# Retention, sparse attention and experts on one core: the norms' inverse roots multiplied behind the products, other work inside the norms, ten expert slots

## The chip, the cores and the metric

The kernel runs on one core of a Trainium2 chip. The metric is the device time of one execution in microseconds (us); the kernel before takes 2245.85 us, the median of three runs. A core has TensorE (PE; its weight loads are shown apart, as PEld), VectorE (DVE), ScalarE (ACT), GpSimd (POOL) and SyncE (SP), which run side by side and wait for one another on semaphores. SP and ACT also issue the transfers; all of these share 16 DMA engines.

## What is computed

Two blocks over 256 tokens of width 1024, everything in float32. The first has a retention mixer, a gated feed-forward layer (FFN), a sparse-attention mixer with shared keys and values, and a second FFN. The second has a gated mixer (a spatial branch and a windowed attention that also reads 256 context tokens), and 16 experts that each take 32 tokens. Every layer is wrapped in norms:

```python
h = x
for layer in range(2):
    if layer == 1:
        shared = nsa_shared_kv(h, kv_norm, ...)        # rms_norm(h, kv_norm) @ kv_w
    normed = rms_norm(h, mix_norm_pre[layer])
    mixed = retention_mixer(normed, ...) if layer < 1 else nsa_mixer(normed, ..., shared)
    h = h + rms_norm(mixed, mix_norm_post[layer])
    normed = rms_norm(h, ffn_norm_pre[layer])
    gate, up = split(normed @ w_in)
    h = h + rms_norm((silu(gate) * up) @ w_out, ffn_norm_post[layer])
...
h1 = modulate(rmsnorm(x, norm1_g), sh1, sc1); hc = modulate(rmsnorm(ctx, norm1_g), csh1, csc1)
x = x + g1 * ((g_a * (y_a @ w_proj_a) + g_b * (y_b @ w_proj_b)) @ w_out)
h2 = modulate(rmsnorm(x, norm2_g), sh2, sc2)
x = x + g2 * expert_choice_ffn(h2, w_router, w_gate, w_up, w_down)   # 16 x 24 MB of weights
```

`rms_norm(x, g)` is x * rsqrt(mean(x*x)) * g over the 1024 features of a token.

## The kernel before, in words

Features lie on the 128 partitions in 8 chunks of 256 tokens, so a sum over features is a product with a matrix of ones: `norm(n)` is 8 float32 products of `sq` with `ones` into bank 4 of PSUM. ACT takes the root (`roots`), DVE the reciprocal (`inverse`, into `rs`).

Dense weights come in units of 1 MB (`load`) through a ring of six slots (`RING`), issued by SP in order. Each unit is split into two rounded halves for the fast matmul: ACT copies (`split_hi`), DVE subtracts (`split_lo`), with two buffers each; a ring slot is free when its low half is made, a split buffer when PE has finished the unit (`used`). Tokens are split the same way into `x_hi` and `x_lo`. A unit is then 48 matmuls: `col_products` (with `col_T`, `col_tok`) for columns of a weight, line 616 of the profile; `wide_tok` (24 matmuls of 512 columns, line 640); `row_T` for rows of a weight, line 653, which accumulates 8 output chunks in four PSUM banks.

A seam between two layers runs as `post` and `pre`: squares of the four PSUM banks, `norm`, root, reciprocal, `xn` = product * gain * `rs` (DVE), `h += xn` (POOL, `residual`, line 2039), squares of `h`, `norm`, root, reciprocal, `xn` = h * gain * `rs`, the split of `xn`, and only then the first product of the next layer. This happens at N_POST0/N_PREF0, N_POSTF0/N_PRE1, N_POST1/N_PREF1 (where the context's norm N_CTX stands between the two) and N_POSTF1/N_IN2.

An FFN has 11 steps of three units: gate and up columns, and the rows of the output weight of the step before. ACT takes silu from PSUM, DVE multiplies by up (`hidden`), and both split the result into `f_hi`, `f_lo`, one pair for all steps. The eight steps in the middle are a hardware loop.

In the second block the mixer's products are ordered v, u (`ua`), q, keys (unit 12, for own tokens and context), then the spatial products, then values (unit 13). Keys are copied across partitions by 8 small DMAs (`kd2`, line 1460) before the windowed attention; its gates are computed inside the attention. Then `w_proj_a` (PA), `w_proj_b` (PB), the gated sum (POOL adds, line 2059) and `w_out` (WO), the router, the choice of tokens (`xe`) and the experts.

The experts' weights are 192 loads of 2 MB (`load_expert`) through `ERING` = 8 slots: seven can be issued before the tokens are chosen, the eighth (`late_expert_slots`, whose last part lies over the split operands) after the last product that reads those. From then on load g waits until PE has used load g - 8 (`e_used`).

Small tables (a bias table of 3 MB written to DRAM with each row repeated 128 times, `bias_skew`; norm gains; router weights) are moved by ACT's queue.

## Time and profile before

| | us |
|---|---|
| three runs | 2242.27, 2245.85, 2246.39 |
| the profiled execution, its own time | 2246.82 |
| its span | 2245.0 |
| PE busy / DVE / ACT / POOL | 1707.0 / 675.8 / 577.4 / 135.2 |
| 0 to 1310 us | the dense layers, 1 MB weight units |
| 1310 to 2227 us | the experts |

An execution's time is the span and 1.8 us around it. The profile has a page (busy time of each engine, the span in 40 slices, the DMA queues, the chain of work that ended last), and the trace behind it can be asked for a stretch, an engine or a line. TensorE's granted clock is given as a share of 2.4 GHz: 1.00 is that level, 0.50 is 1.2 GHz. "<-" names what ended an idle time.

### The profile page before, as it was taken

How to read it: one execution, taken by the hardware profiler on the slowest of the kernel's cores; microseconds unless marked ns; L12 is line 12 of the kernel's file. 1: busy time of each engine (PE TensorE's matmuls, PEld its weight loads, DVE VectorE, ACT ScalarE, POOL GpSimd, SP SyncE). 2: the span in 40 equal slices, each digit the busy share in tenths (PEclk: the TensorE clock that was granted, in tenths of full speed). 3: DMA queues.
4: the chain of work that ended last, by engine and by line, in shares of the span. 5: the costliest groups of instructions: out<-in, count | busy, mean ns of one | idle time of the engine just before them, and what ended most of it. 6: DMA issues, size and time to landing. Idle time of an engine off the chain costs nothing.

```text
span 2245.0 us, 27132 instructions
## 1 busy us (share of the span) xinstructions
PE 1707.0 (76%) x11760; PEld 1186.1 (53%) x11760; DVE 675.8 (30%) x973; ACT 577.4 (26%) x962; POOL 135.2 (6%) x153
## 2 busy tenths in 40 slices
PE   7998899979888999697888665566565555656655
PEld 7898799968557999595678631111111111111111
DVE  4644454454546444462555310000000000000001
ACT  3354344433654343341554210000000000000000
POOL 1101100010221000100321000000000000000000
PEclk8999899979999999898999788887878787888778
DMA  9843455528582555353126269999999999999995
GB/s 233 271 148 113 159 170 186 187 76 245 215 309 93 182 176 187 112 169 94 57 76 241 116 278 428 427 428 428 428 428 428 427 427 428 429 426 428 429 427 246
DMA packets 160620, 603.54 MB, mean 269 GB/s; under 512 B 9542, under 2 KB 114151, under 8 KB 132711
## 3 DMA queue, kind: packets, MB, share of 16 engines
q1 hardware_dynamic: 147712, 587.23, 66.9%
q10 hardware_dynamic: 12808, 14.85, 3.1%
q8 instruction: 79, 1.29, 0.2%
q14 instruction: 21, 0.17, 0.0%
HBM read 594.71 MB, written 4.19 MB: 267 GB/s over the span
## 4 chain that ended last, share of the span: by engine, by line
PE 51%; DMA 38%; DVE 5%; ACT 3%; POOL 1%; issue 1%; ACTq 0%; DVEq 0%
PE ps L616 20%; DMA late_expert_slots<-in_w_exp_down 13%; DMA late_expert_slots<-in_w_exp_gate 13%; PE ps L653 12%; DMA late_expert_slots<-in_w_exp_up 11%; PE ps L640 3%; PE ps L1133 3%; PE ps L600 2%; DVE split_operands L538 2%; PE ps L995 1%; PE ps L1154 1%; POOL residual L2039 1%; DVE inv_root L1567 1%; PE ps L804 1%; PE ps L983 1%
## 5 line engine op out<-in xcount | busy, mean ns | idle before, releaser
L616 PE MATMUL ps<-split_operands 128*128 128x256 f32 x3744 | 466.1, 287 | 18.8 <-DVE split_operands L561 14.4
L616 PEld LDWEIGHTS ps<-split_operands 128*128 128x128 f32 x3744 | 460.8, 194 | 21.8 <-issue 21.0
L538 DVE TENSOR_TENSOR split_operands<-dense_ring,split_operands 128x1024 fp32r<-128x1024 f32 x288 | 353.4, 1269 | 352.0 <-ACT split_operands L530 352.0
L530 ACT ACTIVATE split_operands<-dense_ring 128x1024 fp32r<-128x1024 f32 x288 | 288.1, 1050 | 286.0 <-PE ps L653 161.1
L2007 DVE TENSOR_TENSOR arena<-arena,ps 128x512 f32<-128x512 f32 x16 | 11.0, 688 | 870.8 <-PE ps L1133 870.8
L1133 PE MATMUL ps<-late_expert_slots,arena 128*32 128x512 f32 x768 | 131.0, 817 | 103.9 <-DMA late_expert_slots<-in_w_exp_gate 53.6
L1133 PE MATMUL ps<-dense_ring,arena 128*32 128x512 f32 x768 | 125.6, 789 | 80.3 <-DMA dense_ring<-in_w_exp_gate 41.9
L653 PE MATMUL ps<-split_operands 128*128 128x256 f32 x1152 | 148.5, 294 | 26.4 <-DVE split_operands L548 17.6
L653 PEld LDWEIGHTS ps<-split_operands 128*128 128x128 f32 x1152 | 147.3, 203 | 28.5 <-issue 15.5
L653 PE MATMUL ps<-hidden_split,split_operands 128*128 128x256 f32 x1056 | 134.4, 289 | 8.4 <-DVE split_operands L538 8.4
L653 PEld LDWEIGHTS ps<-hidden_split,split_operands 128*128 128x128 f32 x1056 | 132.2, 196 | 8.8 <-issue 8.8
L1133 PEld LDWEIGHTS ps<-late_expert_slots,arena 128*32 128x32 f32 x768 | 24.6, 129 | 205.0 <-DMA late_expert_slots<-in_w_exp_gate 84.7
L1133 PEld LDWEIGHTS ps<-dense_ring,arena 128*32 128x32 f32 x768 | 25.5, 130 | 180.3 <-issue 77.2
L1154 PE MATMUL ps<-dense_ring,arena 128*32 128x512 f32 x384 | 68.2, 846 | 47.2 <-DMA dense_ring<-in_w_exp_down 44.8
L1154 PE MATMUL ps<-late_expert_slots,arena 128*32 128x512 f32 x384 | 63.2, 791 | 52.6 <-DMA late_expert_slots<-in_w_exp_down 52.6
L1553 ACT ACTIVATE arena<-ps 128x512 f32<-128x512 f32 x16 | 9.6, 597 | 301.3 <-PE ps L1154 301.3
L600 PE MATMUL ps<-squares,ones 128*128 128x256 f32 x192 | 59.0, 471 | 35.0 <-ACT squares L1180 35.0
L1547 ACT ACTIVATE arena<-ps 128x512 f32<-128x512 f32 x16 | 9.6, 597 | 291.3 <-PE ps L1133 291.3
L1551 ACT ACTIVATE arena<-ps 128x256 f32<-128x256 f32 x16 | 6.1, 383 | 298.4 <-PE ps L1139 298.4
L640 PE MATMUL ps<-split_operands 128*128 128x512 f32 x288 | 67.2, 395 | 6.9 <-DVE split_operands L561 6.9
L600 PEld LDWEIGHTS ps<-squares,ones 128*128 128x128 f32 x192 | 44.0, 237 | 47.9 <-ACT squares L1180 33.0
L1133 PE MATMUL ps<-dense_tables,arena 128*32 128x512 f32 x256 | 41.5, 779 | 35.4 <-DMA dense_tables<-in_w_exp_up 20.7
(272 smaller groups left out, 1599.9 us busy)
## 6 DMA issues: line engine op xcount, KB each, us to landing
dense_ring<-in_w_exp_gate SPq DMA_DIRECT2D x24, 2048.0 KB, 36.7
dense_ring<-in_w_exp_up SPq DMA_DIRECT2D x24, 2048.0 KB, 36.1
late_expert_slots<-in_w_exp_up SPq DMA_DIRECT2D x24, 2048.0 KB, 36.7
dense_ring<-in_w_exp_down SPq DMA_DIRECT2D x24, 2048.0 KB, 36.0
late_expert_slots<-in_w_exp_gate SPq DMA_DIRECT2D x24, 2048.0 KB, 35.9
late_expert_slots<-in_w_exp_down SPq DMA_DIRECT2D x24, 2048.0 KB, 36.4
dense_ring<-in_ffn_w_in SPq DMA_DIRECT2D x44, 1024.0 KB, 5.1
dense_ring<-in_ret_w_in SPq DMA_DIRECT2D x24, 1024.0 KB, 11.9
```

The lines of the kernel that those rows point to most:

```text
L530: act.activation(w_hi[:, n % 2, c], ring[U % RING][:, c], ACT.Copy).then_inc(hi_ready, 1)
L538: dve.tensor_tensor(w_lo[:, n % 2, c], ring[U % RING][:, c], w_hi[:, n % 2, c], ALU.subtract).then_inc(lo_ready, 1)
L600: mm = pe.matmul(ps[:, 4, 0:T], ones[:], sq[:, c, :], start=c == 0, stop=c == 7)
L616: mm = pe.matmul(ps[:, bank, b * T:b * T + T], left, right, start=k == 0 and i == 0, stop=k == 7 and i == 2)
L640: mm = pe.matmul(ps[:, banks[t], :], x[:, 4 * half + k, t * P:t * P + P], w[:, k, :], start=half == 0 and k == 0 and i == 0, stop=half == ...
L653: mm = pe.matmul(ps[:, bank0 + b // 2, (b % 2) * T:(b % 2) * T + T], w[:, c, b * P:b * P + P], v[:, c, :], start=first and c == 0 and i == ...
L804: mm = pe.matmul(ps[0:60, kind, 0:T], blocks[:, kind, 8 * w + c, :], slot8(U)[:, c, :], start=w == 0 and c == 0, stop=w == 1 and c == 7)
L983: mm = pe.matmul(ps[:, 5 + 2 * s, t * T:t * T + T], src[:, k, t * P:t * P + P], slot8(U_IN2 + 13)[:, k, :], start=k == 0, stop=k == 7)
L995: mm = pe.matmul(ps[:, 7, b * T:b * T + T], w[:, k, b * P:b * P + P], x[:, k, :], start=k == 0 and i == 0, stop=k == 7 and i == 2)
L1133: mm = pe.matmul(ps[32 * j:32 * j + 32, bank, :], xcur[:, k, :], sl[:, c, 512 * j:512 * j + 512], start=k == 0, stop=k == 7)
L1154: mm = pe.matmul(ps[32 * g:32 * g + 32, 6, :], e_hidT[:, m * P + 32 * (w - 8):m * P + 32 * (w - 8) + 32], sl[:, m, 512 * half:512 * half + ...
L1567: dve.reciprocal(rs[:], root[:]).then_inc(rs_ready, 1)
```

## The change

- **Inverse roots behind the products.** x_hi and x_lo are made from h * gain (`tokens_hi`, `gained_lo`), without the inverse root. The next layer's first two units start on them, interleaved by chunk (`pair_products`), and `norm(n)` stands between the first and second half of the second unit. The inverse root is multiplied where the products leave PSUM: into the rotation tables, the retention's gates (`g_scale`) and values (by token, `rs_tok`, after `turn_rs`), in the FFNs once on the gate ahead of silu (`gate`) and once on its result (`silu_scale`), and on keys and values (`kv_out`). This holds for N_PRE0, N_PREF0, N_PRE1 and N_PREF1; N_IN2 and N_MOE stay as they were.
- **Shorter norms.** Squares of a PSUM bank and the last updates of h start bank by bank (`acc_done`) during the last unit. DVE adds to h (`post`), no longer POOL. The retention's output product starts while the last head's norm runs, in banks 5, 6, 7, 4. The last hidden step of an FFN is split into `x_hi`/`x_lo` and so doesn't wait for `f_hi`.
- **Other work inside norms.** The two halves of the bias tables' products (`bias_table`), the context's sum of squares and the context's keys and values (`keys(ctxn)`, `values(ctxn)`) run on PE inside the seams. The context's norm itself runs on POOL during the second FFN. The bias table's write to DRAM and six small loads are issued during the first FFN (`small_loads`).
- **Order of the second mixer**: v, keys, values, u with the spatial products inside, q. The keys' DMAs are issued two units before q. The last rotation of q runs after the first scores. DVE makes the gated sum by bank.
- **Ten expert slots**: `ERING` = 10, three in the arena. Loads 2 to 8 go out at the points in the diff.

```diff
-ERING = 8
+ERING = 10
...
+ACC = {N_POST0: (5, 6, 7, 4), N_POSTF0: (4, 5, 6, 7), N_POST1: (0, 1, 2, 3), N_POSTF1: (0, 1, 2, 3)}
+TOLD = {N_POST0: 0, N_POSTF0: 3, N_POST1: 6, N_POSTF1: 9, U_PB: 12, U_WO: 15}
+SUM_BANK = {N_PRE0: 4, N_POST0: 0, N_PREF0: 4, N_POSTF0: 0, N_PRE1: 4, N_POST1: 4, N_PREF1: 0, N_POSTF1: 4,
+            N_IN2: 4, N_MOE: 4, N_END: 4}
...
+        e_slots = [arena_slots[0], ring_tail[:], arena_slots[1], ring_mem[:, 0, :], arena_slots[2]] + \
+            [ring_mem[:, i, :] for i in (1, 2)] + [late_slots[:, i, :] for i in range(3)]
...
+                    sp.wait_ge(xhi_ready, X_PA + 4)
+                    sp.wait_ge(xlo_ready, X_PA + 4)
+                    load_expert(2)
+            sp.wait_ge(lo_ready, 2 * SPLIT_NO[U_PB + 3] + 2)
+            load_expert(3)
+            sp.wait_ge(merged, 4)
+            load_expert(4)
+            for g, U in ((5, U_WO + 1), (6, U_WO + 3)):
                 sp.wait_ge(lo_ready, 2 * SPLIT_NO[U] + 2)
                 load_expert(g)
             sp.wait_ge(used, U_END)
-            for g in range(5, ERING - 1):
+            for g in range(7, ERING - 1):
                 load_expert(g)
             sp.wait_ge(xe_mm, 8)
             load_expert(ERING - 1)
...
+            def pair_products(U, banks, place, x0, between):
+                def chunk(v, k):
+                    hi, lo = parts_of(U + v)
+                    if k % 4 == 0:
+                        pe.wait_ge(lo_ready, 2 * SPLIT_NO[U + v] + k // 4 + 1)
+                    for b in range(2):
+                        for i, (w, x) in enumerate(((hi, x_hi), (hi, x_lo), (lo, x_hi))):
+                            left, right = place(b, w[:, k, :], x[:, k, :])
+                            mm = pe.matmul(ps[:, banks[v], b * T:b * T + T], left, right,
+                                           start=k == 0 and i == 0 and b == 0, stop=k == 7 and i == 2,
+                                           skip_group_check=True)
+                    return mm
+                for k in range(4):
+                    pe.wait_ge(xlo_ready, x0 + k + 1)
+                    chunk(0, k)
+                    chunk(1, k)
+                for k in range(4, 8):
+                    pe.wait_ge(xlo_ready, x0 + k + 1)
+                    mm = chunk(0, k)
+                mm.then_inc(used, 1)
+                between()
+                for k in range(4, 8):
+                    mm = chunk(1, k)
+                mm.then_inc(used, 1)
...
+                    if last and b in (1, 3, 5):
+                        mm.then_inc(acc_done, 1)
...
+            for u in range(8):
+                row_pair(U_RO, u, 8, X_RO, ACC[N_POST0], ((g_sc, 7), None, (g_sc, 8), (oroot, 4)))
+            norm(N_POST0)
             pe.wait_ge(on_ev, 4)
...
+                pair_products(U0, (gate_bank(f, 0), gate_bank(f, 0) + 1), by_feature, x0, lambda: norm(n))
...
+            pair_products(U_KV, (1, 3), by_feature, X_KV, lambda: norm(N_PRE1))
...
+            pe.wait_ge(ctx_squared, 1)
+            for c in range(8):
+                mm = pe.matmul(ps[:, 6, 0:T], ones[:], ctx_sq[:, c, :], start=c == 0, stop=c == 7)
+            mm.then_inc(ctx_sum, 1)
...
+            pe.wait_ge(ctx_ready, 2)
+            take(U_K)
+            keys(ctxn, 7).then_inc(kc_mm, 1)
             norm(N_IN2)
+            take(U_V)
+            values(ctxn, 6).then_inc(vc_mm, 1)
...
+            def tokens_hi(posted, name):
+                for k in range(DC):
+                    if posted is not None:
+                        act.wait_ge(h_ready, POST[posted] + k + 1)
+                    act.activation(x_hi[:, k, :], h[:, k, :], ACT.Copy, scale=col(name, k)).then_inc(xhi_ready, 1)
+                    if k % 2:
+                        act.activation(sq[:, k - 1:k + 1, :], h[:, k - 1:k + 1, :], ACT.Square).then_inc(sq_ready, 1)
...
+            def small_loads():
+                act.wait_ge(brow_ev, 1)
+                act.dma_start(bias_dram, bias_rows.unsqueeze(1).to_broadcast([HEADS, P, 384])).then_inc(bias_out, 16)
+                for dst, src in rests:
+                    act.dma_start(dst, src).then_inc(rest_in, 16)
...
+            def gained_lo(x0, name, k):
+                dve.wait_ge(xhi_ready, x0 + k + 1)
+                dve.scalar_tensor_tensor(out=x_lo[:, k, :], in0=h[:, k, :], scalar=col(name, k), in1=x_hi[:, k, :],
+                                         op0=ALU.mult, op1=ALU.subtract).then_inc(xlo_ready, 1)
...
+            def post(n, name, U, x0=None, next_name=None):
+                split_lo(dve, U)
+                split_lo(dve, U + 1)
+                inverse(n)
+                for k in range(11 if next_name else 9):
+                    if k < 8:
+                        dve.scalar_tensor_tensor(out=xn[:, k, :], in0=acc_chunk(ACC[n], k), scalar=col(name, k),
+                                                 in1=rs[:], op0=ALU.mult, op1=ALU.mult).then_inc(scaled, 1)
+                    if 1 <= k < 9:
+                        dve.wait_ge(scaled, POST[n] + k)
+                        dve.tensor_tensor(h[:, k - 1, :], h[:, k - 1, :], xn[:, k - 1, :],
+                                          ALU.add).then_inc(h_ready, 1)
+                    if next_name and k >= 3:
+                        gained_lo(x0, next_name, k - 3)
...
+                def gate(j, r=0):
+                    taken(dve, gate_unit(f, j), r)
+                    dve.tensor_tensor(halves(f_silu[:, j % 2, :]), halves(ps[:, gate_bank(f, j), :]), two(rs[:]),
+                                      ALU.mult).then_inc(f_gate, 1)
+                def silu_scale(j, r=0):
+                    dve.wait_ge(f_act, r * 2 + (base + j + 1))
+                    dve.tensor_tensor(halves(f_silu[:, j % 2, :]), halves(f_silu[:, j % 2, :]), two(rs[:]),
+                                      ALU.mult).then_inc(f_sc, 1)
...
+            dve.wait_ge(gt_sig, 2)
+            product_b(0)
+            product_b(1)
+            merge(0)
+            product_b(2)
+            merge(1)
+            pair_lo(dve, X_WO, 0, two_chunks(gb, 0))
+            product_b(3)
...
+                if k % 2 == 0:
+                    bank_of(U_WO, k // 2)
...
```

## Rows read from the trace of the kernel before

**Rows 1.** Table by stretch: busy us (instructions) of PE, PEld, DVE, ACT, POOL; clock, DMA share, GB/s.

```profile
300.00:400.00 100.00, 100.00 (x835) 100.00 (x834) 47.72 (x46) 40.17 (x46) 0.00 (x0) 1.00 0.55 179
...
1290.00:1300.00 10.00, 3.26 (x11) 2.80 (x12) 8.49 (x22) 0.00 (x0) 0.00 (x0) 0.50 0.00 0
...
1400.00:1500.00 100.00, 58.18 (x368) 14.91 (x372) 2.76 (x4) 2.95 (x6) 1.49 (x4) 0.82 1.01 428
```

**Rows 2.** Experts: the chain's last load (start, us, what); SP's issues of three loads.

```profile
2186.93 36.27 DMA late_expert_slots<-in_w_exp_down
...
1262.10 47.23 SPq L446 DMA_DIRECT2D late_expert_slots<-in_w_exp_up  x3
```

**Rows 3.** Timeline, start: start us, us, engine, line, what, [idle before].

```profile
18.95 2.00 ACT L530 ACTIVATE split_operands<-dense_ring 128x1024 fp32r<-128x1024 f32 x2 [9.96 <-DMA dense_ring<-in_ret_w_in]
20.97 1.28 ACT L1186 ACT_TABLE_LOAD   x1
22.27 0.38 ACT L1186 ACTIVATE root<-ps 128x256 f32<-128x256 f32 x1
...
31.72 47.69 PE L616 MATMUL ps<-split_operands 128*128 128x256 f32 x384 [4.32 <-issue]
```

**Rows 4.** Timeline, seam between the retention's heads and its output product.

```profile
189.71 1.89 PE L745 MATMUL ps<-squares,ones 128*128 128x256 f32 x8
200.40 48.48 PE L653 MATMUL ps<-split_operands 128*128 128x256 f32 x384 [8.80 <-DVE split_operands L538]
```

**Rows 5.** Timeline, seam to the first FFN.

```profile
249.57 3.72 PE L600 MATMUL ps<-squares,ones 128*128 128x256 f32 x16 [0.69 <-ACT squares L1180]
255.53 3.23 DVE L1655 SCALAR_TENSOR_TENSOR normed<-ps,cols,inv_root 128x256 f32<-128x256 f32 x8
270.68 26.29 PE L616 MATMUL ps<-split_operands 128*128 128x256 f32 x192 [4.00 <-DVE split_operands L561]
```

**Rows 6.** Timeline, last output unit of the first and of the second FFN.

```profile
462.45 8.50 PE L653 MATMUL ps<-hidden_split,split_operands 128*128 128x256 f32 x48 [4.21 <-DVE split_operands L538]
...
904.21 7.47 PE L653 MATMUL ps<-hidden_split,split_operands 128*128 128x256 f32 x48 [4.21 <-DVE split_operands L538]
```

**Rows 7.** DMA queues from 33 to 63 us: packets, MB, share of 16 engines.

```profile
q10 hardware_dynamic: 1873, 2.88, 85.2%
q1 hardware_dynamic: 998, 1.02, 9.6%
```

**Rows 8.** Timeline, shared keys and values: shift DMAs, the blocks made from them, the next products.

```profile
509.49 4.33 ACTq L1342 DMA_DIRECT2D arena<-arena  x6
522.83 3.75 DVE L1710 TENSOR_TENSOR arena<-arena,cols 128x480 f32<-128x480 f32 x4
530.39 14.02 PE L804 MATMUL ps<-dense_ring,arena 128*60 128x256 f32 x64
```

**Rows 9.** Timeline, seam to the second FFN.

```profile
713.59 25.13 PE L616 MATMUL ps<-split_operands 128*128 128x256 f32 x192 [6.45 <-DVE split_operands L561]
```

**Rows 10.** Timeline, second mixer: v, context keys, first scores, their maximum, first transposes.

```profile
936.18 23.47 PE L640 MATMUL ps<-split_operands 128*128 128x512 f32 x96 [6.88 <-DVE split_operands L561]
1015.01 7.07 PE L959 MATMUL ps<-arena,dense_ring 128*128 128x256 f32 x32
1057.04 2.08 PE L1005 MATMUL ps<-arena 64*128 64x512 f32 x4 [14.73 <-DMA arena<-arena]
1060.92 1.23 DVE L1889 TENSOR_TENSOR arena<-ps,tabs 128x1024 f32<-128x1024 f32 x1 [26.22 <-PE ps L1007]
```

**Rows 11.** Timeline, from PB over the merge and WO to the router's norm.

```profile
1222.03 2.48 DVE L1933 TENSOR_TENSOR arena<-arena,ps 128x512 f32<-128x512 f32 x4 [2.31 <-PE ps L653]
1230.30 8.58 PE L653 MATMUL ps<-split_operands 128*128 128x256 f32 x48 [8.38 <-DVE split_operands L548]
1243.08 18.98 PE L653 MATMUL ps<-split_operands 128*128 128x256 f32 x144 [4.20 <-DVE split_operands L548]
1267.94 1.75 DVE L1567 RECIPROCAL inv_root<-root 128x256 f32<-128x256 f32 x1 [2.61 <-ACT root L1186]
```

## What I predicted

> **What bounds the kernel now.** I read the busy table by stretch first. From 300 to 400 us PE is busy all the time at a granted clock of 1.00 (2.4 GHz) while DMA is at 0.55: the dense layers are bound by PE. From 1400 to 1500 us PE is at 58% and DMA at 1.01 with 428 GB/s: the experts are bound by their weights [rows 1]. The chain of waits says the same, and that the last load lands at 2223.2 [rows 2]. So a gain before 1310 us moves the whole expert stream forward, and a gain inside it comes only from loads made earlier. Then I read PE's timeline for idle time in the dense part: it stands at the seams [rows 3 to 11]. A unit at full clock is 5.76 us (48.49 for 8 units, less a slow start; 5.74 to 5.77 in the chain). R below is the end of PE's last product before a seam; hand-overs between engines cost 0.02 to 0.1 us and are in the steps.
>
> **Start.** Before, products start at 31.7, after the norm and the bias tables, and eight units take 47.69, which is 1.7 over 46.0 (half clock at first), so unit 2 starts at 44.9 [rows 3]. After: the weights land at about 18 to 19 as before, two units are split by 22 to 24, PE starts at 22.6, does 72 matmuls (8.6, and 2 of low clock) and the norm of 3.7 [rows 5] to 36.2 to 37, then the second half (2.9). The inverse (root 0.4, reciprocal 1.75), the tables' multiplication (0.9), a split (2.4) and a rotation (1.5) follow the norm, so unit 2 starts at 43.5, with a low clock after 4.4 idle (1.7) and a transposition of 0.3: about 45.5. Loss 0.6; bounds +3 and -3.
>
> **Retention heads.** `g_scale` (0.7) goes ahead of each silu. The path from a gate unit's end to the next head's output product is then 8.6 to 8.8 us (scale, silu, split, table load 1.28, root, reciprocal 1.75, multiplication 1.23) where PE has 8.9 of other work. Loss 0.5, bounds 0 and 2.
>
> **Output product of the retention.** The last head's norm leaves 8.80 idle and 48.48 for 46.05 of work [rows 4]. After, the first two pairs are split before that norm, and bank 4 comes last, so the norm (root 6 us after the last gate unit) is behind 4.3 us of products and two units. 11.5 less; 10 if bank 4 is waited for.
>
> **First FFN's seam.** Before, R is 248.88 and four units are done at 296.97, R + 48.1 [rows 5]. After: squares of three banks lie inside the last unit, norm to R + 3.75, root and reciprocal to R + 6.0. DVE then runs product (0.40, 8 in 3.23 [rows 5]), addition (0.37) and low half (0.40) for each chunk, so the first low half is there at R + 9.1 and the next every 1.17, less than the 1.44 PE needs for two chunks. The first half of the bias tables (15 small products and one; an estimate of 3 us, bounded by 6.5 at half clock) fills R + 3.8 to 7. The pair with the norm inside takes 11.5 + 3.75 and 1 for low clock: R + 25.3, four units R + 36.8. Gate scale, silu, second scale, up and split of step 0 end at R + 32, ahead of the first output unit at R + 36.8. 11.3 less; bounds 8 (half clock for all of the first chunks) and 13.
>
> **FFN steps.** Each gets two DVE operations of 0.7 more, 9.8 of DVE per 17.3. The low half of an output unit is ready 3.4 after the gate unit, 2.3 before PE wants it. Nothing.
>
> **FFN ends.** The last output unit waits 4.21 and takes 8.50 or 7.47 for 5.76 [rows 6]. The last hidden step no longer waits for the unit before, and is split 1.8 before it is wanted. 6.95 and 5.9 less.
>
> **The bias write inside the first FFN.** From 33 to 63 us this write's queue (q10) takes 85% of the DMA engines and the weights' queue gets 1.02 MB, one unit in 30 us [rows 7]. It survived because six units had landed. After, it is issued at about R + 45, when six units ahead of PE have landed; unit 12 lands at about R + 80 and is wanted, split, at R + 82.9. Six small loads follow in the same queue. I take 1, bounds 0 and 8. The Trainium skill, "DMA: Bandwidth & Descriptors", Queues, rings and completion order, says that each DMA engine goes round the queues packet by packet; by that the weights would have got as many packets as the write, and this would cost nothing. The rows don't agree: 998 packets against 1873 with four loads waiting.
>
> **Shared keys and values.** Before, their next products start at 530.4, R + 59.4 with R = 470.95 [rows 6, 8]. After, the pair is done at R + 25.5, then unit, transposition, unit, a wait of 1.3 for `kv_out` behind `pre`, two units: R + 50.2. The shift DMAs are issued from P + 8 to P + 13.5 (P is the pair's end, 0.7 each); blocks are made 9 after the last issue as before, and take 3.75 [rows 8]: P + 26.4, R + 51.9. 7.6 less; bounds 4 (the bias read of 2 MB ahead of them in the queue) and 9.5.
>
> **Second FFN's seam.** R = 689.94, four units before at 738.72, R + 48.8 [rows 9]. After, as in the first, with the context's sum (3.7) as filler: R + 36.5. 12.3 less; bounds 9 and 13.5. The context's squares on ACT fall while PE is on the first output unit.
>
> **Second mixer.** R = 911.68. The maximum of the first scores starts at 1060.9, R + 149.2, after 14.73 idle for the keys' DMAs [rows 10]. After: keys of the context to R + 10.7, norm to 14.4 (the last squares are at 13.1), values to 21.3; modulated tokens arrive at R + 21.4. From there PE has v 21.9, keys and values 13.8 (7 each [rows 10]), eight units 46.1, spatial 3.6, four turns 3.5, scores 2.1, half a gate unit 2.9, a turn 0.9: 94.8. Each split on the way is ready in time, the nearest by 1.5, and the keys' DMAs by 14. But the last rotation (2.2) stands ahead of the maximum on DVE: R + 118.5. 30.7 less: 14.7 the DMAs, 13.8 context products now inside the norm, 3.1 an earlier start, 1.7 clock, less 2.6 for the rotation in front. Bounds 24 and 33.
>
> **Merge and output.** PB ends at 1222.0, WO at 1262.06, with 8.38 and 4.20 idle and 27.6 for 23.0 of work [rows 11]. After, three banks are multiplied and two added inside PB's last unit; the first split pair is ready at +1.7, unit 2 at +7: end at +24.7. 15.4 less; bounds 12 and 17. The router's norm starts on banks: inverse at W + 4.25 (W is WO's end) instead of 5.9. 1.6 less. The router's own chain (to 1310) stays.
>
> **Ten slots.** The eighth load is issued at 1309.3 [rows 2]; from 1290 to 1300 DMA moves nothing [rows 1]. Up to the last landing, 185 loads take 913.9 us, 4.94 each. After it is 183: 9.9 less. If the two more aren't landed in time it is 0; against that speak 35 idle us, hence 8 to 9.9.
>
> **Sum.** -0.6 - 0.5 + 11.5 + 11.3 - 1 + 6.95 + 5.9 + 7.6 + 12.3 + 30.7 + 15.4 + 1.6 + 9.9 = 111. The steps take every hand-over at its best, so I take 3 off: 108 from the profiled execution's 2246.8 is 2138.8. The median of the runs stands 1.0 below it: 2138.
>
> The Trainium skill, "ScalarE: Activation LUTs", What ACT_TABLE_LOAD costs, adds a drain of about 1.38 us to each 1.28 of a table switch. At the start the root follows its load by 0.02 [rows 3], so I count none. By the page three seams, where the root's load now ends only 0.25 after the norm, would each be 1.4 later, and the time 2142.
>
> **Rivals.**
> (a) The weights starve: if fewer than six units have landed when the bias write starts, each one missing is worth up to 5.8 of PE, and the small loads add some. 2144 to 2152. For: the margin of 3. Against: the same depth sufficed at the start. Chance 0.12.
> (b) The new DVE order sets the pace: splits queue behind waiting scales, rotations and merges, and low clock returns at each seam. Taking the low bounds of the seams (8, 4, 9, 24, 12) the sum is 25 lower: 2150 to 2165. For: eleven waits are new in DVE's queue. Against: DVE is at 48% [rows 1]. Chance 0.2.
> (c) The extra slots bring nothing because the stream's start is set by the last slot: 2147. Chance 0.05.
> (d) Slower than before: in the FFN steps gate, silu, second scale and up become a chain that PE waits for. There are 22 steps; from 4.9 us per step it eats the 108. PE waited for none of it in 300 to 400 us, and 2.3 or more are free at each step. 2250 to 2290, chance 0.02.
> (e) More than I count, with fewer low-clock stretches: 2115 to 2126. Chance 0.06.
> Forecast, 2126 to 2148: 0.55.
>
> **Numbers.** The range 2122 to 2158 leaves out (d), half of (b) and part of (e). A run of this kernel can tell about 0.2% from no change; all but (d) and some mishap are far below that: faster 0.97, same 0.01, slower 0.02.
>
> **What would show it.** Idle ahead of the first output unit of the retention under 1; four FFN units done at R + 37; no idle ahead of an FFN's last unit; no wait on DMA in PE's rows for the first FFN (else (a)); scores' maximum at R + 118; WO's end 25 after PB's; nine loads issued ahead of the choice of tokens, 4.94 each after. I'm wrong if PE waits on DVE rows for scales, or if the expert stream's first release isn't about 100 us earlier.

## The result and the profile after

The changed kernel takes 2167.6 us (median of four runs, 2165.1 to 2172.3) against 2246.0 before: ratio 0.966, interval 0.9636 to 0.9678. It is faster by 78 us where I had forecast 108, and it lies 10 us above my range of 2122 to 2158. Its profiled execution took 2165.05 with a span of 2163.3; the numbers below are of that one.

I first laid the two timelines side by side by the steps of the prediction. R is again the end of TensorE's (PE's) last product ahead of a seam.

| stage | predicted gain | measured gain |
|---|---|---|
| start, to the end of the query and key units | -0.6 | +2.3 |
| retention heads | -0.5 | 0.0 |
| retention's output product | 11.5 | 10.3 |
| first FFN's seam | 11.3 | 10.6 |
| first FFN behind it, its end included | 6.95 - 1 | **-21.7** |
| shared keys and values | 7.6 | 8.8 |
| second FFN's seam | 12.3 | 11.4 |
| second FFN behind it | 5.9 | 3.6 |
| second mixer, to the merge | 30.7 | 29.9 |
| merge and output | 15.4 | 15.4 |
| norm and choice of the router | 1.6 | 3.4 |
| experts | 9.9 | 9.8 |
| tail | 0 | -2.1 |
| sum | 111 - 3 | 81.7 |

Twelve of the thirteen lines are within 3 us of the forecast. One is off by 28, and that is the whole miss; the other twelve come to 103.4 for 105.1. (The sum is the difference of the two spans, 2245.0 - 2163.3.) The seams look as they were worked out. These are PE's rows of the changed kernel, at the retention's output product and the first FFN's seam (start us, us, engine, line, what, [idle before]); they answer to [rows 4, 5]:

```profile
201.44 34.81 PE L731 MATMUL ps<-split_operands 128*128 128x256 f32 x288 [0.65 <-DVE split_operands L581]
236.09 3.61 PE L639 MATMUL ps<-normed_and_squares,ones 128*128 128x256 f32 x16
...
245.06 10.85 PE L684 MATMUL ps<-split_operands 128*128 128x256 f32 x72 [0.16 <-DVE split_operands L1718]
255.74 3.61 PE L639 MATMUL ps<-normed_and_squares,ones 128*128 128x256 f32 x16
259.01 3.22 PE L684 MATMUL ps<-split_operands 128*128 128x256 f32 x24
262.07 11.68 PE L662 MATMUL ps<-split_operands 128*128 128x256 f32 x96
```

The idle 8.80 is 0.65 now. Behind R = 236.3 the four units are done at 273.75, R + 37.5, where I had R + 36.8; the norm's sum (3.61) stands inside the products. The second mixer and the output product, which answer to [rows 10, 11]:

```profile
889.67 7.07 PE L1024 MATMUL ps<-arena,dense_ring 128*128 128x256 f32 x32
896.57 3.62 PE L639 MATMUL ps<-normed_and_squares,ones 128*128 128x256 f32 x16
900.03 7.07 PE L1031 MATMUL ps<-dense_ring,arena 128*128 128x256 f32 x32
...
995.83 1.13 PE L1096 MATMUL ps<-arena 64*128 64x512 f32 x4
...
1168.16 23.30 PE L731 MATMUL ps<-split_operands 128*128 128x256 f32 x192 [1.45 <-DVE split_operands L581]
```

The context's products (7.07 each) lie around the norm's sum, the scores at 995.83 no longer wait for the keys' DMAs (14.73 before), and the output product has 1.45 of idle time for 8.38 and 4.20.

Then the first FFN. The stretch 300 to 400 us, in which PE was busy for all of 100.00 at a clock of 1.00 [rows 1], now reads (busy us and instructions of PE, PEld, DVE, ACT, POOL; clock, DMA share, GB/s):

```profile
300.00:400.00 100.00, 81.96 (x671) 81.96 (x672) 47.55 (x49) 35.20 (x40) 0.00 (x0) 0.89 0.61 175
```

PE's timeline has the hole, and it names a VectorE (DVE) split as what ended it:

```profile
318.04 7.38 PE L731 MATMUL ps<-hidden_split,split_operands 128*128 128x256 f32 x48 [27.01 <-DVE split_operands L571]
```

The last releaser need not be the cause, so I went back one engine more. ScalarE (ACT) in the same stretch; ACTq is its sequencer issuing DMAs:

```profile
279.75 0.68 ACTq L1437 DMA_DIRECT2D bias_skew<-arena  x1
280.46 8.10 ACTq L1439 DMA_DIRECT2D dense_tables<-in_nsa_w_in  x1
...
288.60 22.75 ACTq L1439 DMA_DIRECT2D dense_tables<-in_cmp_w_k  x2
...
313.26 0.98 ACTq L1439 DMA_DIRECT2D sink<-in_attn_sink  x1
314.54 2.00 ACT L563 ACTIVATE split_operands<-dense_ring 128x1024 fp32r<-128x1024 f32 x2 [32.40 <-issue]
```

The bias write itself is issued in 0.68 us. The six small loads behind it take ScalarE 33.8 us to issue, and from 282.1 to 314.5 it does no work and makes no high halves for PE. The chain of waits in this stretch (start, us, what) goes through the issues and not through any weight:

```profile
288.60 12.60 ACTq L1439
301.23 10.12 ACTq L1439
...
314.54 1.06 ACT split_operands L563
```

In the kernel before, the same six were issued from 253.7 on, where no bias write was under way, in 0.41 to 0.60 us each; the first:

```profile
253.72 0.41 ACTq L1280 DMA_DIRECT2D dense_tables<-in_nsa_w_in  x1
```

The hole costs 27.0 of idle time and 1.6 of low clock behind it (7.38 for a unit of 5.76): 28.6. The 6.95 at this FFN's end did come, hence -21.7. Without the hole the median would be 2139.

### The profile page after: what moved, and what is told of

Its sections match the earlier page's. It is cut to its first block, busy times and chain, and to the rows that moved or that the text cites. A ratio compares the mean times of both kernels' runs of the same rounds, so it can differ in the third digit from the quotient of the medians.

```text
span 2163.3 us, 27150 instructions
## 1 busy us (share of the span) xinstructions
PE 1676.8 (78%) x11764; PEld 1163.9 (54%) x11764; DVE 708.9 (33%) x1020; ACT 579.4 (27%) x959; POOL 111.1 (5%) x123
## 4 chain that ended last, share of the span: by engine, by line
PE 49%; DMA 39%; DVE 5%; ACT 3%; ACTq 1%; issue 1%; POOL 1%; SPq 0%; DVEq 0%
PE ps L662 18%; DMA dense_tables<-in_w_exp_gate 13%; DMA dense_tables<-in_w_exp_up 13%; DMA dense_tables<-in_w_exp_down 13%; PE ps L731 12%; PE ps L716 3%; PE ps L684 2%; PE ps L1224 2%; DVE split_operands L571 2%; PE ps L639 1%; PE ps L1085 1%; ACTq L1439 1%; PE ps L1245 1%; ACT split_operands L563 1%; DMA dense_ring<-in_ret_w_in 1%
## 5 line engine op out<-in xcount | busy, mean ns | idle before, releaser
L662 PE MATMUL ps<-split_operands 128*128 128x256 f32 x3360 | 413.9, 284 | 6.6 <-DVE arena L1776 4.1
L662 PEld LDWEIGHTS ps<-split_operands 128*128 128x128 f32 x3360 | 407.9, 193 | 8.1 <-issue 4.6
L1224 PE MATMUL ps<-dense_ring,arena 128*32 128x512 f32 x624 | 101.2, 781 | 77.0 <-DMA dense_ring<-in_w_exp_gate 39.5
L1224 PE MATMUL ps<-late_expert_slots,arena 128*32 128x512 f32 x592 | 104.7, 843 | 71.4 <-DMA late_expert_slots<-in_w_exp_gate 36.4
L731 PE MATMUL ps<-split_operands 128*128 128x256 f32 x1248 | 154.1, 286 | 7.2 <-DVE split_operands L581 7.2
L731 PEld LDWEIGHTS ps<-split_operands 128*128 128x128 f32 x1248 | 152.7, 195 | 9.0 <-issue 6.4
L1224 PE MATMUL ps<-arena 128*32 128x512 f32 x624 | 96.4, 745 | 62.0 <-DMA arena<-in_w_exp_gate 35.2
L731 PE MATMUL ps<-hidden_split,split_operands 128*128 128x256 f32 x960 | 120.0, 285 | 27.8 <-DVE split_operands L571 27.8
L731 PEld LDWEIGHTS ps<-hidden_split,split_operands 128*128 128x128 f32 x960 | 118.0, 194 | 28.2 <-DVE split_operands L571 28.2
L1224 PEld LDWEIGHTS ps<-dense_ring,arena 128*32 128x32 f32 x624 | 20.0, 127 | 153.4 <-DMA dense_ring<-in_w_exp_up 54.5
L1224 PEld LDWEIGHTS ps<-late_expert_slots,arena 128*32 128x32 f32 x592 | 19.5, 133 | 150.6 <-DMA late_expert_slots<-in_w_exp_up 52.6
L1224 PEld LDWEIGHTS ps<-arena 128*32 128x32 f32 x624 | 20.5, 123 | 132.9 <-issue 69.0
L1245 PE MATMUL ps<-arena 128*32 128x512 f32 x304 | 51.1, 805 | 34.3 <-DMA arena<-in_w_exp_down 28.8
L1245 PE MATMUL ps<-late_expert_slots,arena 128*32 128x512 f32 x320 | 51.6, 777 | 33.6 <-DMA late_expert_slots<-in_w_exp_down 31.2
L684 PE MATMUL ps<-split_operands 128*128 128x256 f32 x384 | 55.9, 312 | 23.3 <-DVE split_operands L571 18.6
L1245 PE MATMUL ps<-dense_ring,arena 128*32 128x512 f32 x288 | 47.0, 784 | 29.9 <-DMA dense_ring<-in_w_exp_down 28.3
```

The costliest lines, as they stand in the source:

```text
L662: mm = pe.matmul(ps[:, bank, b * T:b * T + T], left, right, start=k == 0 and i == 0, stop=k == 7 and i == 2)
L684: mm = pe.matmul(ps[:, banks[v], b * T:b * T + T], left, right, start=k == 0 and i == 0 and b == 0, stop=k == 7 and i == 2, skip_group_che ...
L731: mm = pe.matmul(acc_chunk(banks, b), w[:, c, b * P:b * P + P], v[:, c, :], start=first and c == 0 and i == 0 and b % 2 == 0, stop=last an ...
L1224: mm = pe.matmul(ps[32 * j:32 * j + 32, bank, :], xcur[:, k, :], sl[:, c, 512 * j:512 * j + 512], start=k == 0, stop=k == 7)
L1245: mm = pe.matmul(ps[32 * g:32 * g + 32, 6, :], e_hidT[:, m * P + 32 * (w - 8):m * P + 32 * (w - 8) + 32], sl[:, m, 512 * half:512 * half + ...
```

## Experiments

All ratios are to the kernel before, run on the same chip in turn; the interval is 95%. Two kernels that did not run in the same turn are compared by their medians, and their ratios can put the difference up to 2.8 us elsewhere; where a trace settles a size, it is given. "The small loads first" is the base of most of the later runs.

### What holds the issue

**The small loads first.**

```diff
 def small_loads():
+    for dst, src in rests:
+        act.dma_start(dst, src).then_inc(rest_in, 16)
     act.wait_ge(brow_ev, 1)
     act.dma_start(bias_dram, ...).then_inc(bias_out, 16)
-    for dst, src in rests:
-        act.dma_start(dst, src).then_inc(rest_in, 16)
```

> The changed kernel with one edit: ScalarE issues the six small loads (gate, compression and router weights, sink) ahead of the bias write and not behind it. In the changed kernel TensorE is idle for 27.0 us at 318.04, behind a VectorE step that waits for ScalarE, and ScalarE's own queue shows the bias write issued at 279.75 and the six small loads behind it until 313.3, two of them at 22.75 us together where before they took 0.4 to 0.6 us each. Theory A, ScalarE is held while it issues a load behind the bias write's many small packets: with nothing behind the bias write the 28.65 us are back, 2167.6 - 28.7 = 2139 us (ratio to before 0.952 to 0.953), no idle time over 3 us between 280 and 320, the six issues 0.4 to 1 us each. Theory B, the FFN's weights starve in the DMA queues under the bias write (my rival a of the prediction): the order of ScalarE's issues is no matter, an idle time of 20 to 30 us stays there, on the weights' wait, and the time stays at 2160 to 2168.

Measured: 2137.4 us, ratio 0.9533 (0.9517 to 0.9549). ScalarE's issues in this kernel:

```profile
280.69 0.40 ACTq L1437 DMA_DIRECT2D dense_tables<-in_nsa_w_in  x1
...
283.32 0.89 ACTq L1437 DMA_DIRECT2D sink<-in_attn_sink  x1
284.25 0.68 ACTq L1439 DMA_DIRECT2D bias_skew<-arena  x1
```

None of ScalarE's issues takes 1 us, PE has no idle time in this FFN, and the part behind the seam takes 167.04 us for 195.67. Theory A holds and B falls: the same bytes are issued within 5 us of the same time, and only the order of seven instructions differs.

**Two loads behind it**, the sink (8 KB) and one compression weight (64 KB), the other four ahead.

> As the run with the small loads first, but the two smallest in bytes of them (the sink and the second compression weight of the values) stay behind the bias write. What holds the issue is then told apart. Theory A1, the hold lasts until the bias write's own packets have room again, whatever comes behind: the first of the two is held some 8 to 30 us, and the time is 2150 to 2168. Theory A2, the hold goes by what the loads themselves bring (in the changed kernel the sink behind five others took 0.98 us, the four weight loads 8 to 12 each): the two are issued in under 5 us together and the time is 2139 to 2144. Theory B: 2160 to 2168 with the idle time on the weights' wait.

Measured: 2149.6, ratio 0.9590 (0.9569 to 0.9612).

```profile
282.58 0.94 ACTq L1439 DMA_DIRECT2D bias_skew<-arena  x1
283.56 12.38 ACTq L1441 DMA_DIRECT2D sink<-in_attn_sink  x1
295.97 3.95 ACTq L1441 DMA_DIRECT2D cmp_w_v<-in_cmp_w_v  x1
```

A1 holds by the hold; the time is 0.4 us under its range. The sink took 0.98 as the last of six and takes 12.38 as the first, longer than the 192 KB load in the same place of the changed kernel (8.10): the size of the load that is held matters less than how lately the bias write was issued. Some 16 us of hold leave 11.96 of idle time on PE.

**The kernel before, with its six small loads right behind its own bias write at the start** (they were issued 223 us later).

```diff
     act.dma_start(bias_dram, ...).then_inc(bias_out, 16)
+    for dst, src in rests:
+        act.dma_start(dst, src).then_inc(rest_in, 16)
     ...
-    for dst, src in rests:
-        act.dma_start(dst, src).then_inc(rest_in, 16)
```

> The kernel before with one edit: its six small loads, issued there at 253.7 to 257.0 in 0.4 to 0.6 us each, are issued right behind the bias write at the start (30.3), as the changed kernel does it later. Theory A: ScalarE is held there for 25 to 33 us, a stretch in which it has the start's evictions and activations to do, TensorE idles for most of it, and the time is 2246 + 15 to 30 = 2261 to 2276 us (ratio 1.007 to 1.013); small loads of 0.4 to 0.6 us each would refute it. Theory B: no hold of the issues, the weights of the start are late by at most some us, time 2243 to 2250.

Measured: 2277.6, ratio 1.0158 (1.0141 to 1.0174), 36 us slower than before. That is more than I had put down, and A's mechanism:

```profile
30.75 11.63 ACTq L1220 DMA_DIRECT2D dense_tables<-in_nsa_w_in  x1
42.42 20.11 ACTq L1220 DMA_DIRECT2D dense_tables<-in_cmp_w_k  x2
...
67.89 42.72 PE L616 MATMUL ps<-split_operands 128*128 128x256 f32 x336 [28.79 <-DVE split_operands L538]
```

The hold (34.7 us) is not a matter of this change's other parts: it came at both places where the six stood behind this write.

**The bias write issued by GpSimd (POOL)**, at nearly the same point (275.8 for 279.8); ScalarE's six loads stay where the change has them.

```diff
-    act.dma_start(bias_dram, ...).then_inc(bias_out, 16)
+pool.wait_ge(f_hidden, 2)
+pool.dma_start(bias_dram, ...).then_inc(bias_out, 16)
```

> The changed kernel with one edit: the bias write is issued by GpSimd at the same point of the first FFN, and ScalarE issues its six small loads where it did, now not behind it in its own queue. Theory A3, only the queue that took the bias write is full: ScalarE's issues take 0.4 to 0.9 us each, no idle time of TensorE at 280 to 320, time 2137 to 2140 (ratio 0.952 to 0.954). Theory A4, the hold comes from the 16 DMA engines themselves, which are busy with the bias write's small packets whoever issues them: ScalarE is held again for 10 to 30 us and the time is 2150 to 2168.

Measured: 2165.9, ratio 0.9641 (0.9622 to 0.9660), with 24.45 of idle time on PE. A3 falls; the time is in A4's range, and the hold of 31.8 us just over A4's 30. ScalarE's issues, with nothing large in its own queue:

```profile
280.29 0.40 ACTq L1437 DMA_DIRECT2D dense_tables<-in_nsa_w_in  x1
280.73 4.06 ACTq L1437 DMA_DIRECT2D dense_tables<-in_cmp_w_k  x1
284.82 3.89 ACTq L1437 DMA_DIRECT2D dense_tables<-in_cmp_w_k  x1
288.73 18.77 ACTq L1437 DMA_DIRECT2D cmp_w_v<-in_cmp_w_v  x1
```

From 282 to 312 us the queues of this kernel were (packets, MB, share of 16 engines; q0 is GpSimd's, q1 SP's, q10 ScalarE's):

```profile
q0 software_dynamic: 602, 2.68, 85.0%
q1 hardware_dynamic: 1118, 1.13, 10.7%
q10 hardware_dynamic: 1078, 0.21, 3.4%
```

The write keeps the engines busy from any queue, and of the six loads' some 3040 small packets (the 3088 of the next expectation count 48 of other loads) only 1078 are moved in these 30 us, so they wait in ScalarE's queue: the first is issued in 0.40, the fourth only in 18.77. The Trainium skill, "DMA: Bandwidth & Descriptors", Issuing engines are not separate DMA queues, says that DMAs of different issuers run on the same 16 DMA engines whoever started them, and that issuing from several engines saves only the issuer's own time; by that, moving the write to GpSimd can't free them, and the trace agrees (2165.9 for 2167.6).

**The same with only the two loads beside it**, the other four ahead of the FFN.

> The changed kernel with the bias write issued by GpSimd, four of the small loads issued by ScalarE ahead of the FFN, and only the sink and the second compression weight (384 small packets of some 3088) issued by ScalarE beside the bias write. With the bias write in GpSimd's queue all six behind it held ScalarE for 31.8 us, and with it in ScalarE's own queue these two alone held it for 16.3. Theory A5, an issue is held when ScalarE's own queue is full of packets that are not yet taken, and the bias write in any queue makes that emptying slow: the few packets of these two find room, they take 0.4 to 1 us each, and the time is 2137 to 2140, ratio 0.952 to 0.954. Theory A4, any issue beside the bias write is held: ScalarE is held for 10 to 20 us and the time is 2146 to 2156.

Measured: 2137.0, ratio 0.9533 (0.9516 to 0.9550), the time of "the small loads first".

```profile
280.10 0.35 ACTq L1437 DMA_DIRECT2D sink<-in_attn_sink  x1
280.48 3.81 ACTq L1437 DMA_DIRECT2D cmp_w_v<-in_cmp_w_v  x1
```

A5 holds for the time, and A4, under which ScalarE would be held for 10 to 20 us, falls: few packets find room, and the same two loads that were held for 16 us behind the write in one queue are issued in 4.2 beside it. It is off in one number: the second issue took 3.81 and not 1. Such a 3.8 to 4.1 is there in the run before too. Why the second issue takes it with so little queued stays open.

So what the runs show together is this. ScalarE is held while it issues a DMA when the bias write's packets, or many small ones, stand ahead of it in its own queue, and beside the bias write these go slowly, whoever issued that write. That the queue is then full is my reading; no row shows how full a queue is. SyncE is held too: with the small loads first it takes 11.63 us, from 307.17, to issue one weight unit, and beside GpSimd's write 19.45, from 289.31, where it takes 0.37 elsewhere. TensorE hardly notices that (no idle time in the first case, 1.12 us in the second), since SyncE issues units well ahead of their use.

### What the seams' gains are made of

**Both FFNs' first products behind the inverse again**, on the base of the small loads first.

```diff
-    pair_products(U0, ..., x0, lambda: norm(n))
+    pe.wait_ge(scaled, POST[(N_POST0, N_POST1)[f]] + 8)
+    norm(n)
+    pe.wait_ge(rs_ready, n + 1)
+    pair_products(U0, ..., x0, lambda: None)
```

The first added line makes the sum wait until DVE has read the accumulators, because it goes into one of their banks. A form without that line, from which 6.4 us a seam were expected, let the sum write a bank that DVE still reads; it has no time. On ScalarE the root, and on DVE the inverse, go ahead of the split behind them.

> The kernel with the small loads first, with the products of both FFNs' first two units put behind the norm's sum, root and inverse again (the products' operand itself is still not multiplied by the inverse). At the first FFN the products began at 246.0. The sum now waits until the accumulators are read (some 249.8), takes 3.6 us, the root comes at some 254.4, the inverse ends at 256.5, and the 3.4 us of the sum no longer stand between the products: 256.5 - 246.0 - 3.4 = 7.1 us, and the same at the second, so 2137.4 + 14 = 2151.6 (2147 to 2157), ratio 0.958 to 0.962. That is what putting the inverse behind the products is worth by itself, of the 10.6 and 11.4 us that the two seams gained. If the early start was hidden by the VectorE splits behind it, the time is under 2141.

Measured: 2152.0, ratio 0.9596 (0.9581 to 0.9610): 14.5 us for two seams, 14 expected. PE at the first of them:

```profile
249.05 5.86 PE L639 MATMUL ps<-normed_and_squares,ones 128*128 128x256 f32 x16 [4.17 <-DVE normed_and_squares L1731]
257.17 11.77 PE L684 MATMUL ps<-split_operands 128*128 128x256 f32 x96 [2.26 <-DVE inv_root L1696]
```

In the traces the seams are 6.5 and 6.7 longer. So multiplying the inverse behind the products is worth some 7 us a seam, of 10.6 and 11.4. The rest would then be the operand's own multiplication, which this kernel doesn't bring back, and the new order inside the norm; no run takes these two apart.

**The context's keys and values behind the wide products** and not around the second mixer's norm, on the base of the best kernel below (2123.8 us).

```diff
-    keys(ctxn, 7).then_inc(kc_mm, 1)
     norm(N_IN2)
-    values(ctxn, 6).then_inc(vc_mm, 1)
     for u in range(4):
         wide_tok(U_IN2 + u, ...)
+    keys(ctxn, 7).then_inc(kc_mm, 1)
+    values(ctxn, 6).then_inc(vc_mm, 1)
     pe.wait_ge(kc_ev, 1)
...
```

Their own waits, and ScalarE's copies of their results, move with them.

> The kernel with the sum ahead at the start (2123.8 us, ratio 0.9467), with one part of the change undone: the second mixer's keys and values of the context, 7.07 us each with some 0.1 of overlap, are computed behind the two wide products and not around its norm. If they fill a stretch in which TensorE would only wait for the modulated tokens (the norm's squares end at 863.1 whatever stands ahead of them, the first wide product begins at 871.2), the 13.8 us come back whole: 2137.6 (2136 to 2139), ratio 0.952 to 0.954. If they delayed the norm or what follows where they stand now, less: each us of the difference is that delay. If the stage's end is set by VectorE or by the keys' DMAs and not by TensorE, next to nothing: 2124 to 2128.

Measured: 2139.8, ratio 0.9548 (0.9531 to 0.9565), 16.1 more; 13.8 were expected.

```profile
852.80 6.27 PE L639 MATMUL ps<-normed_and_squares,ones 128*128 128x256 f32 x16 [5.24 <-ACT normed_and_squares L1270]
865.89 24.75 PE L716 MATMUL ps<-split_operands 128*128 128x512 f32 x96 [6.81 <-DVE split_operands L594]
```

The products had filled 5.24 and 6.81 of waiting, so the 13.8 came back whole. What I left out is the clock: after idle time the sum takes 6.27 for 3.62, so that the wide products begin 1.1 us later behind the first sum, and they take 24.75 for 22.03: a further 3.9. From the norm ahead of this stage to the output products both profiles differ by 19.1. Elsewhere the second is 6 to 8 us shorter, in stretches of low clock that shift from one execution to the next.

**Eight expert slots**, on the base of the small loads first.

```diff
-ERING = 10
+ERING = 8
```

> The kernel with the small loads first, with eight expert slots in place of ten (the last two are left out, the order of the others and their early loads stay). The stage of the experts is bound by its loads, one in 4.57 us in the kernel before; two loads fewer stand ahead of it. By my step of 9.9 us the time is 2137.4 + 9.1 to 9.9 = 2146.5 to 2147.3, ratio 0.957 to 0.958. Rival (c), slots bring nothing: 2137.4.

Measured: 2145.5, ratio 0.9563 (0.9548 to 0.9578): 8.1 in the medians. In the profiles it is 9.5: from the first expert product to the last load's landing 912.6 (1210.50 to 2123.11) against 903.1. The slots bring what two loads made earlier bring, and rival (c) falls. (The expectation's 4.57 us for a load is not in the rows; the prediction's 4.94 is, 913.9 for 185.)

### The second FFN's missing 2.4 us

At 728 to 745 GpSimd does the second context's norm, which the change put there; PE waits twice beside it, 1.86 together. DVE and GpSimd of the changed kernel:

```profile
729.62 5.40 DVE L571 TENSOR_TENSOR split_operands<-dense_ring,split_operands 128x1024 fp32r<-128x1024 f32 x2 [0.40 <-ACT split_operands L563]
734.95 2.38 DVE L1836 TENSOR_TENSOR arena<-arena,inv_root 128x512 f32<-128x512 f32 x1
737.45 0.69 DVE L1842 TENSOR_TENSOR arena<-arena,ps 128x512 f32<-128x512 f32 x1
...
731.19 2.75 POOL L2279 TENSOR_TENSOR arena<-arena,mod_gain 128x1024 f32<-128x1024 f32 x1
```

Two splits take 5.40 for 2.36, the scale 2.38 for 0.68. The product at 737.45, of which one operand is in PSUM (ps), takes its usual 0.69.

**GpSimd's steps on one of each four chunks.** The kernel leaves out three quarters of this norm.

> The changed kernel, with GpSimd's three steps on the second context's norm done on one chunk of each four only, so that three quarters of this norm are left out and the context's values with them. In the changed kernel VectorE operations with two operands in SBUF are stretched beside those steps (5.40 us for what took 2 to 3 elsewhere at 728 to 743), and TensorE waits there. Theory C, GpSimd and VectorE hinder each other at SBUF: with a quarter of GpSimd's work some 2 us of the second FFN's 169.4 are back (167.0 to 167.8), and the time is 2165 to 2166, ratio to before 0.964 to 0.965. Theory D, something else stretches them (the low clock, ScalarE): the second FFN stays at 169.4 within 0.3 and the VectorE operations at 730 to 743 keep their lengths.

Measured: 2161.8, ratio 0.9649 (0.9631 to 0.9666). The ratio is C's; the time is 3 us under C's, but the kernel before was 4 us faster in this turn too. What decides is the trace: the second FFN is 2.37 shorter, and the scale takes 1.22. C holds and D falls. The Trainium skill, "SBUF — State Buffer", SBUF: two separate sides, says that GpSimd and a DVE operation with both inputs in SBUF take turns at one pair of ports, and the later of the two is blocked for the whole of the other's instruction. The trace agrees: only operations of that kind are long, and here by 1.7, less than one whole GpSimd step of 2.75.

**The six steps one FFN step apart** (base: the small loads first).

```diff
+    pool.wait_ge(f_hidden, PAIRS + 3 + 3 * q + i)
     pool.tensor_tensor(c, c, v.to_broadcast([P, 4, T]), op)...
```

> The kernel with the small loads first (2137.4 us, ratio 0.9533), with one more edit: GpSimd's six steps on the second context's norm, which ran back to back at 702.8 to 719.4, now wait for one step of the second FFN each, 17.3 us apart. Each step still hinders the VectorE operations beside it (5.40 us for two splits that take 2.36 alone), but a pair of splits has 3.4 us of idle time behind it at this place. Theory C1, the stretch costs only where stretched operations follow each other: the second FFN falls from 169.40 to 167.05 us and the time to 2135.1, ratio 0.952 to 0.953. Theory C2, each step costs TensorE its share wherever it stands (2.35 / 6 = 0.4 us each): no change, 2137.4. The keys' product on the context waits for the last of the six, at some 807, and begins at 864.

Measured: 2134.6, ratio 0.9508 (0.9493 to 0.9523).

```profile
711.92 4.38 DVE L571 TENSOR_TENSOR split_operands<-dense_ring,split_operands 128x1024 fp32r<-128x1024 f32 x2 [0.40 <-ACT split_operands L563]
```

The splits beside a step are still long (4.38 for 2.36), PE no longer waits, and the second FFN takes 167.04 for 169.40. C1 holds: the 2.36 are whole in the trace. The medians alone, 2.8 apart with intervals of the ratio that overlap, wouldn't show it.

### The start, and a faster kernel

The start gained 2.3 where I had -0.6, and its rows show that more is there. PE in the kernel with the small loads first:

```profile
17.39 1.62 PE L684 MATMUL ps<-split_operands 128*128 128x256 f32 x6 [17.39 <-DVE split_operands L571]
...
30.46 3.61 PE L639 MATMUL ps<-normed_and_squares,ones 128*128 128x256 f32 x16
...
41.04 8.02 PE L662 MATMUL ps<-split_operands 128*128 128x256 f32 x48 [4.09 <-DVE arena L1776]
```

At every other seam the norm's sum has to stand inside the products, since its squares come late. Here the squares are done at 14.6 and PE waits for weights until 17.4.

**The first norm's sum ahead of the products** (base: the spread steps).

```diff
-    pair_products(U_RET, ..., X_RET, lambda: norm(N_PRE0))
+    norm(N_PRE0)
+    pair_products(U_RET, ..., X_RET, lambda: None)
...
-    split_hi(act, U_RET + 1)
     roots(N_PRE0)
+    split_hi(act, U_RET + 1)
...
```

On VectorE the first unit's rotation goes ahead of the next split.

> The kernel with GpSimd's steps spread (2134.6 us, 0.9508), with one more edit at the start: the first norm's sum goes ahead of the first two units' products, where TensorE waits for weights until 17.4 anyway, in place of between them, the root goes between the two splits on ScalarE, and the first unit's rotation goes ahead of the next split on VectorE. In the changed kernel the sum stood at 30.0 to 33.6, the root came at 33.7, and TensorE waited 4.09 us at 40.6 for the rotation that needs the inverse. Now the inverse is there at some 23, the 3.6 us of the sum lie in the wait for the weights, and the third unit begins at 34 to 36 in place of 40.6 to 42: 5 to 7 us, time 2128 (2126 to 2131), ratio 0.948. If the weights' landings set the pace of this stage (one unit in 3 us beside a unit of 5.8 us of products: they do not by the rows), nothing changes.

Measured: 2123.8, ratio 0.9467 (0.9451 to 0.9483), 10.8 less than its base (9.2 by the ratios); 5 to 7 were expected.

```profile
10.00 5.90 PE L639 MATMUL ps<-normed_and_squares,ones 128*128 128x256 f32 x16 [10.00 <-ACT normed_and_squares L1290]
17.41 0.97 PE L684 MATMUL ps<-split_operands 128*128 128x256 f32 x6 [1.51 <-DVE split_operands L571]
20.91 12.56 PE L684 MATMUL ps<-split_operands 128*128 128x256 f32 x90 [2.52 <-DVE split_operands L571]
33.33 1.68 PE L662 MATMUL ps<-split_operands 128*128 128x256 f32 x12
```

The third unit begins at 33.33 for 41.04, and without the 4.09 of idle time PE has less at low clock behind it: the query and key units end at 68.9 for 77.9, 9.0 earlier. The last 1.8 are within what one execution differs from the next. This kernel beats the changed one by 44 us and is 5.3% faster than before.

## Why the prediction was wrong, point by point

- **The step that failed** is "The bias write inside the first FFN": "Six small loads follow in the same queue. I take 1, bounds 0 and 8." It measured 28.6, and the runs showed in its place ScalarE held for 33.8 us at those six issues: with them ahead of the write the 28.6 are gone. I had priced only the weights' queue, from what the DMA engines did [rows 7], and not what the issuing engine does meanwhile, though the change puts six issues behind this write on the engine that makes every high half. The trace of before could not show it, because there nothing was issued behind the write for 223 us; it did show 0.4 to 0.6 for each issue elsewhere. With no row of a DMA issued behind a large one, the bound should have been the write's own 35 us in the queue, not 8.
- **Rival (a)** put a loss at the right place with the wrong mechanism. The weights did get little from 282 to 312 (packets, MB, share of 16 engines; q10 has the write, q1 the weights):

```profile
q10 hardware_dynamic: 1938, 2.98, 86.2%
q1 hardware_dynamic: 929, 0.95, 8.9%
```

But six units had landed and PE never waited for one, and with the small loads first it has no idle time in this FFN at all. The Trainium skill, "DMA: Bandwidth & Descriptors", Queues, rings and completion order, has each DMA engine go round the queues packet by packet; if its packets are the profile's, these two counts would be equal, and as in [rows 7] they are not.

- **What the rest was worth:** the kernel with the small loads first takes 2137.4, and the forecast was 2138. That it comes so near is partly luck. The kernel before ran 4 us faster in those turns, so by the ratio the gain is 105 of the 108; and in this kernel start and router gained 1.9 and 1.7 more than their terms, the second FFN 2.3 less. The terms of the seams, the mixer, the merge and the slots held to 1.2 each. The runs that undid parts of them gave 14.5 (13.2 by the traces) for the 14 expected then, 16.1 for the 13.8 of the context's products, and 8.1 (9.5 by the trace) for 9.9. The other signs came as said: 0.65 of idle time for under 1, R + 37.5 for R + 37, the scores' maximum at R + 117.4 for 118, WO's end 24.75 behind PB's.
- **Two sums of mine were off:** 8.80 idle and 48.48 for 46.05 make 11.2 for the retention's output product, not 11.5 (10.3 came). The low bounds that rival (b) names lie 20 under the terms, not 25, which makes 2158 and not 2163; both lie in (b)'s range.
- **Start:** I let the first weights land "at about 18 to 19 as before". They were split from 14.86 on, not 18.95 [rows 3]. The kernel before loads the bucket tables (495 and 49.5 KB) in the same stretch, and the changed one does so later. That these tables were the cause wasn't tried alone.
- **Second FFN:** the "Nothing." of the FFN steps missed that GpSimd's steps stretch DVE's operations there, which cost 2.36; two runs brought it back.
- **Router:** 3.4 for 1.6. The idle 1.63 ahead of the norm's sum is gone; most of the rest is clock (the 32 products at L1184 take 9.31 for 10.38).
- **Tail:** 2.1 lost, the last small product 3.76 for 2.02. In the run with eight slots it took 2.02 again at the same place. The product is the same, so this is clock (0.71 granted over the end, 0.78 before); that it is chance I take from one trace of each.
- **Table loads:** at the start of the best kernel the root follows its load by 0.02 again (16.97 and 1.28, then 18.27), and the seams came out as summed. The drain that the Trainium skill's "ScalarE: Activation LUTs", What ACT_TABLE_LOAD costs, adds to each switch isn't seen.
- **Rivals (b) to (e):** no seam fell near (b)'s low bounds, and what DVE cost is the second FFN's step above; the slots brought 9.8, the FFN steps had no chain (167.04 is 29 units of 5.76), and (e) had no part.
- **The chances:** 0.97 for faster was right. The range was too narrow at its upper end, because bound 8 for a mechanism without a row was a guess and not a bound.

## What to carry to other kernels

A DMA that is moved has two prices: what it does to the other transfers, and how long the engine that issues the next one is held behind it. Put what is small ahead of what is large in an engine's queue, and keep the issues behind a large one off the engine that feeds TensorE. Moving only the large one to another engine brought 2 to 4 us here. A sum or a root that can be ready while TensorE waits for its first weights should not stand between products.

## What the runs showed of the hardware

- One DMA of 3 MB is issued in 0.68 to 0.94 us, and the next small one then takes 8.1 to 12.4 us to issue, six of them 33.8 to 34.7. Issued from GpSimd's queue, the same write still made ScalarE's fourth small load take 18.77, and one of SyncE's weight units 19.45 (beside two small loads).
- The same write showed as 1938 packets with 2.98 MB in ScalarE's queue and as 602 with 2.68 MB in GpSimd's (282 to 312 us of each kernel). In both, the engines were all but fully busy at 98 to 173 GB/s in total while it ran, where the experts' loads reach 427.
- Beside GpSimd steps on SBUF, DVE operations with both inputs in SBUF took 2.38 for 0.68, and those with one in PSUM their usual 0.69. GpSimd's own steps with a gain or a shift took 2.75 back to back beside them and 1.89 when spread.
